# A hybrid decoder layer on one core: start, sample loop and gates reordered, and the last quarter of the second feed-forward product computed in two passes over the tokens

## What is computed

```python
h = rmsnorm(x, norm_mix)
q, k, v, B, C, H, ga, gb = split(h @ w_in)      # 3 x 768, 3 x 512, 2 x 1024 columns
att = dilated_attention(q, k, v, rel_bias)      # 3 groups of 4 heads; samples read caches
b = B * (conv_b + conv3(C * H))
m = sigmoid(ga) * (att @ w_att_out) + sigmoid(gb) * (b @ w_conv_out)
x = x + m @ w_o
x = x + relu(rmsnorm(x, norm_mlp) @ w_ff1) ** 2 @ w_ff2
y = rmsnorm(x, norm_final)
```

## Time and profile before

| | us |
|---|---|
| median of 3 runs | 1695.65 (1692.61 to 1696.15) |
| the profiled execution, its own time | 1697.69 |
| span of the profiled execution | 1695.8 |
| PE busy | 1650.8 (97%) |
| DVE busy | 672.5 (40%) |
| ACT busy | 472.1 (28%) |
| POOL busy | 73.1 (4%) |
| mean granted clock of TensorE | 0.992 of full speed |

### The profile page before, as it was taken

How to read it: one execution, slowest core, us unless ns; L and a number is a source line. 1 busy time by engine, 2 the same in 40 slices (tenths; PEclk the granted TensorE clock), 3 DMA queues, 4 the chain that set the end, 5 groups by cost and what they waited for, 6 DMA issues and landing times.

```text
span 1695.8 us, 28576 instructions
## 1 busy us (share of the span) xinstructions
PE 1650.8 (97%) x10715; PEld 1602.2 (94%) x10715; DVE 672.5 (40%) x1222; ACT 472.1 (28%) x906; POOL 73.1 (4%) x86
## 2 busy tenths in 40 slices
PE   7999999999989999999999999999999999999998
PEld 7999998888978888899999999999999999999998
DVE  6112123344644444323544344333333333333454
ACT  5212123443433443111423331033101321033212
POOL 0430000000000000000122000000000000000011
PEclk9999999999999999999999999999999999999998
DMA  5524554332256765433111111111111111111112
GB/s 174 158 90 129 172 181 123 110 103 85 82 154 171 200 175 147 148 102 108 39 50 37 50 37 50 49 37 49 50 37 49 37 49 40 46 41 46 43 31 106
DMA packets 229017, 152.08 MB, mean 90 GB/s; under 512 B 23870, under 2 KB 219286, under 8 KB 228969
## 3 DMA queue, kind: packets, MB, share of 16 engines
q1 hardware_dynamic: 200412, 120.32, 24.7%
q10 hardware_dynamic: 26268, 28.31, 4.9%
q0 software_dynamic: 2288, 2.80, 0.7%
HBM read 118.32 MB, written 35.43 MB: 91 GB/s over the span
## 4 chain that ended last, share of the span: by engine, by line
PE 86%; issue 3%; DVE 3%; DMA 3%; ACT 2%; SPq 2%; ACTq 1%; DVEq 0%; POOL 0%
PE bank L626 27%; PE bank L627 27%; PE bank L628 27%; ACT wh L1042 1%; PE bank L771 1%; PE bank L740 1%; PE bank L757 1%; PE bank L693 1%; DMA wr<-in_w_conv_out_dram 1%; PE bank L950 1%; DMA xt<-in_x_prompt_dram 1%; DMA xp<-in_x_sample_dram 0%; DMA out_dram<-yt 0%; DMA wr<-in_w_in_dram 0%; SPq L510 0%
## 5 line engine op out<-in xcount | busy, mean ns | idle before, releaser
L626 PE MATMUL bank<-xhi,wh 128*128 128x352 f32 (+1 forms) x1104 | 373.2, 338 | 4.7 <-DVE sga L1811 2.6
L627 PE MATMUL bank<-xlo,wh 128*128 128x352 f32 (+1 forms) x1104 | 362.2, 328 | 0.0
L628 PE MATMUL bank<-xhi,wl 128*128 128x352 f32 (+1 forms) x1104 | 361.8, 328 | 0.0
L1449 DVE TENSOR_TENSOR wl<-wr,wh 128x1024 fp32r<-128x1024 f32 (+1 forms) x134 | 179.7, 1341 | 260.2 <-ACT wh L1042 259.4
L627 PE MATMUL bank<-flo,wh 128*128 128x368 f32 (+1 forms) x768 | 251.7, 328 | 0.0
L627 PE MATMUL bank<-hlo,wh 128*128 128x368 f32 (+1 forms) x768 | 251.4, 327 | 0.0
L626 PE MATMUL bank<-hhi,wh 128*128 128x368 f32 (+1 forms) x768 | 250.6, 326 | 0.3 <-DVE rel L1867 0.3
L626 PE MATMUL bank<-fhi,wh 128*128 128x368 f32 (+1 forms) x768 | 250.5, 326 | 0.0
L628 PE MATMUL bank<-fhi,wl 128*128 128x368 f32 (+1 forms) x768 | 250.1, 326 | 0.0
L628 PE MATMUL bank<-hhi,wl 128*128 128x368 f32 (+1 forms) x768 | 250.1, 326 | 0.0
L1042 ACT ACTIVATE wh<-wr 128x1024 fp32r<-128x1024 f32 (+1 forms) x134 | 136.1, 1015 | 364.8 <-PE bank L628 293.4
(11 more groups left out here) (218 smaller groups left out, 1734.2 us busy)
## 6 DMA issues: line engine op xcount, KB each, us to landing
wr<-in_w_ff_dram SPq DMA_DIRECT2D x64, 512.0 KB, 3.7
wr<-in_w_in_dram SPq DMA_DIRECT2D x46, 512.0 KB, 3.9
d_T<-stg ACTq DMA_DIRECT2D x18, 544.0 KB, 2.8
kvc<-in_cache_kv_g_dram SPq DMA_DIRECT2D x16, 512.0 KB, 5.3
kvc<-in_cache_kv_g_dram SPq DMA_DIRECT2D x32, 256.0 KB, 5.8
d_tm<-tm ACTq DMA_DIRECT2D x12, 512.0 KB, 3.7
d_m<-bb ACTq DMA_DIRECT2D x8, 544.0 KB, 3.0
ml<-d_m SPq DMA_DIRECT2D x8, 544.0 KB, 4.4
```

The costliest lines, as they stand in the source:

```text
L626: pe.matmul(bank[c][:, 0:n], wh[st_.p][:, k, :], a, start=(k == 0), stop=False)
L627: pe.matmul(bank[c][:, 0:n], wh[st_.p][:, k, :], b, start=False, stop=False)
L628: last = pe.matmul(bank[c][:, 0:n], wl[st_.p][:, k, :], a, start=False, stop=(k == nk - 1))
L1449: dve.tensor_tensor(wl[st_.p][:, 0:nk, :], wr[st_.p][:, 0:nk, :], f32(wh[st_.p][:, 0:nk, :]), ALU.subtract).then_inc(w_lo, 1)
```

## The change

Line numbers of the changed kernel are used in the excerpts of its order only; everywhere else a line is one of the kernel before.

**At the start** SP loads the mixing norm's weights as one row of 4 KB. PE spreads it over the partitions by two products of 512 columns with a row of ones that POOL sets (banks 0 and 1), ACT copies one half to `gb` and DVE the other. Three squarings of x move ahead of splits on ACT. The bias tables are multiplied one at a time behind the chunks of step 2, and the constants transposed after chunk 0 of step 3; their copies on ACT and DVE move behind the epilogues of those steps.

```diff
-                sp.dma_start(gb[:], bass.AP(g_mix.tensor, 0, [[0, P], [1, D]])).then_inc(gb_in, 16)
+                sp.dma_start(gb[0:1, :], bass.AP(g_mix.tensor, 0, [[D, 1], [1, D]])).then_inc(gb_in, 16)
...
         keep_warm(WARM[0])
+        pe.wait_ge(gb_in, 16)
+        pe.wait_ge(ones_row, 1)
+        for half in range(2):
+            pe.matmul(bank[half][:], sr[:, 0, :], gb[0:1, 512 * half:512 * half + 512], start=True, stop=True).then_inc(gb_pe, 1)
+        keep_warm(WARM[1])
...
-        tables()
         chunk(Step(1), KD, 2, xhi, xlo)
-        for s in range(2, 6):
+        for c in range(3):
+            chunk(Step(2), KD, c, xhi, xlo)
+            tables(c)
+        chunk(Step(3), KD, 0, xhi, xlo)
+        tables(None)
+        for c in (1, 2):
+            chunk(Step(3), KD, c, xhi, xlo)
...
         square_x(0)
         root_x(0)
+        act.wait_ge(gb_pe, 2)
+        act.activation(gb[:, 0:512], bank[0][:], ACT.Copy).then_inc(gb_c, 1)
         square_x(1)
...
         split_hi(Step(1), KD)
+        square_x(6)
+        square_x(7)
         split_x_hi(3)
-        square_x(6)
+        square_x(8)
         stage_first(0, 0, 1)
         split_x_hi(4)
-        square_x(7)
-        square_x(8)
...
+        dve.wait_ge(gb_pe, 2)
+        dve.tensor_copy(gb[:, 512:D], bank[1][:]).then_inc(gb_c, 1)
+        dve.wait_ge(gb_c, 2)
         scale_x(0)
```

```diff
+                    if g == 2:
+                        pe.wait_ge(cs_ev, 1)
                     pe.wait_ge(pt_d, i * 4 + (8 * g + j))
...
-                pe.wait_ge(s_d, 64)
+                pe.wait_ge(pt_d, 16)
                 for f in range(FC):
-                    last = pe.transpose(bank[3][0:18, f * P:(f + 1) * P], csb[:, f, :], ident[:])
+                    last = pe.transpose(bank[7][0:18, f * P:(f + 1) * P], csb[:, f, :], ident[:])
                 last.then_inc(cs_pe, 1)
-                pe.wait_ge(cs_ev, 1)
...
                     z_terms(f)
+                    bias_scores(g, i, 1)
                 split_lo(st1, KD)
                 prompt_chunk(g, st0, f, 0)
-                bias_scores(g, i, 1)
+                if g < 2:
+                    bias_scores(g, i, 1)
                 prompt_chunk(g, st0, f, 1)
                 bias_scores(g, i, 2)
...
             st0 = Step(S_SAMPLE, (2, b))
+            keys_dve(b, 1)
             split_lo(st0 + 1, KD)
-            keys_dve(b, 1)
...
             query_loads(b)
             gate_b_weights(b)
+            if not last:
+                conv_weights(b + 1)
...
+        def gate(i, p):
+            st_ = Step(S_GATE + 2 * p, (4, i))
+            chunk(st_, KD, 0, xhi, xlo)
+            if isinstance(i, int) and p == 0:
+                turn_sample_out(NB_S - 1)
+            chunk(st_, KD, 1, xhi, xlo)
+            pe.wait_ge(ats_a, 32)
+            pe.wait_ge(res_in[p], i * 32 + 32)
+            pe.wait_ge(res_d, i * 6 + 3 * p)
+            for t in range(TILES):
+                w = rows_of(t)
+                last = pe.transpose(bank[3 + t // 4][:, (t % 4) * P:(t % 4) * P + w], xp[p][0:w, t, :], ident[0:w, 0:w])
+                if t in (3, 7, 8):
+                    last.then_inc(res_pe, 1)
+            chunk(st_, KD, 2, xhi, xlo)
...
             for c, (t0, n) in enumerate(CH):
                 chunk_in(st_, c)
+                if c == 2:
+                    split_hi(st_ + 2, KD)
```

```diff
+        for j in range(KD):
+            weights(W_2[3][:, :, j * P:(j + 1) * P], KD, Step(S_FIRST + j))
+        for j in range(KD):
+            weights(W_2[3][:, :, j * P:(j + 1) * P], KD, Step(S_REST + j))
+            if j >= 5:
+                store(j - 5)
...
+        for j in range(KD):
+            st_ = Step(S_FIRST + j)
+            pe.wait_ge(w_lo, st_.s + 1)
+            for c in range(2):
+                pe.wait_ge(taken[c], st_.s)
+                products(st_, CH_LAST[c], bank[c], (93, 96) if j + c == 0 else None).then_inc(ready, 1 + c)
...
+        pe.wait_ge(taken[1], S_REST)
+        pe.wait_ge(taken[2], S_FIRST)
+        turned = {1: 0, 2: 1, 4: 2, 5: 3, 6: 4, 7: 5}
+        for j in range(KD):
+            st_ = Step(S_REST + j)
+            if j in turned:
+                t = turned[j]
+                pe.wait_ge(yT_d, 2 * KD)
+                if t >= 2:
+                    pe.wait_ge(yt_a, t - 1)
+                    pe.wait_ge(yt_d, t - 1)
+                turn_y(t, range(KD))
+            pe.wait_ge(w_lo, st_.s + 1)
+            if j >= 2:
+                pe.wait_ge(rest_d, j - 1)
+            products(st_, CH_LAST[2], bank[2 - j % 2], None, range(4))
+            if j == KD - 1:
+                pe.wait_ge(ssf_p, 2 * KD - 3)
+                sums(range(FIRST_TILES, TILES), bank[0], ssf, True, False)
+            products(st_, CH_LAST[2], bank[2 - j % 2], None, range(4, KD)).then_inc(ready, 3)
+            if j == 1:
+                pe.wait_ge(ssf_p, KD - 1)
+                pe.wait_ge(taken[0], S_REST)
+                sums(range(FIRST_TILES), bank[6], ssf, True, True).then_inc(yn_pe, 1)
+        pe.wait_ge(yT_d, 3 * KD - 1)
+        pe.wait_ge(rest_d, KD - 1)
+        for t in range(FIRST_TILES, TILES):
+            if t < 8:
+                pe.wait_ge(yt_a, t - 1)
+                pe.wait_ge(yt_d, t - 1)
+            turn_y(t, range(4))
+        pe.wait_ge(sqf_a, 2 * KD)
+        sums(range(FIRST_TILES, TILES), bank[0], sqf[1], False, True).then_inc(yn_pe, 1)
+        pe.wait_ge(rest_d, KD)
+        pe.wait_ge(yT_d, 3 * KD)
+        for t in range(FIRST_TILES, TILES):
+            turn_y(t, range(4, KD))
...
+            dve.tensor_tensor(x, acc[:, 0:n], x, ALU.add).then_inc(y_d, 1)
+            if between:
+                split_lo(between, KD)
+            dve.wait_ge(y_d, e + 1)
+            dve.tensor_scalar(yT[:, j, t0:t0 + n], x, gfc[:, j:j + 1], None, ALU.mult).then_inc(yT_d, 1)
...
+        for j in range(KD):
+            st_ = Step(S_REST + j)
+            t0, n = CH_LAST[2]
+            if j == KD - 1:
+                y_out(5)
+            if j == 2:
+                dve.wait_ge(yn_pe, 1)
+                dve.tensor_scalar(rst[:, 0, 0:FIRST_TILES], bank[6][:, 0:FIRST_TILES], 1.0 / D, EPS, ALU.mult,
+                                  ALU.add).then_inc(yn_d, 1)
+                rstd(yn_d, 1, yr_a, 1, (slice(None), slice(0, FIRST_TILES)))
+            chunk_in(st_, 2)
+            add(j, CH_LAST[2], bank[2 - j % 2], 88 + j).then_inc(rest_d, 1)
+            add_rest(j, t0, n, 88 + j, rest_d, j + 1, st_ + 2 if j + 2 < KD else None)
+            if 2 <= j < KD - 1:
+                y_out(j - 2)
...
+        for j in range(1, KD):
+            pool.wait_ge(sqf_a, j + 1)
+            pool.tensor_tensor(ssf[:, 0:FIRST], sqf[0][:, 0:FIRST] if j == 1 else ssf[:, 0:FIRST], sqf[j % 2][:, 0:FIRST],
+                               ALU.add).then_inc(ssf_p, 1)
...
+            pool.wait_ge(sqf_a, KD + j + 1)
+            pool.tensor_tensor(ssf[:, FIRST:TOK], sqf[0][:, FIRST:TOK] if j == 1 else ssf[:, FIRST:TOK], sqf[j % 2][:, FIRST:TOK],
+                               ALU.add).then_inc(ssf_p, 1)
+            pool.wait_ge(ssf_p, KD - 1 + j)
```

247 lines of the change are left out of this document (132 added, 115 removed).

## The result

| | before | changed |
|---|---|---|
| median, same comparison (us) | 1695.90 (1692.61 to 1697.01, 4 runs) | 1683.04 (1682.76 to 1683.65, 4 runs) |
| ratio | | 0.993 (0.9917 to 0.9944) |
| span of the profiled execution | 1695.8 | 1681.9 |
| PE busy | 1650.8 | 1647.1 |

The change wins 12.9 us at the median and 13.9 in the profiled spans. 1678.9 had been forecast, so 16.8 against 12.9; the time lies inside the range of 1669 to 1688. The page of the changed kernel, part 1, answers to the earlier trace rows: PE's share is 98% now.

What follows compares the result with a forecast made beforehand. It took PE's products as the bound (busy 97% of the span). Its terms, 2.4 - 2.8 - 7.0 - 7.1 - 2.6 + 0.3, made -16.8 us: 1680.9 in the profiled execution's terms, 1678.9 at the median; range 1669 to 1688.

Steps and rivals of the forecast that it cites:

- Third attention group: Third attention group: PE's waits for `cst` and the second score bias go, some given back at the third biases; -2.8 us.
- The entry to the gates: Before the gates: moved chunk covers the late residual, so waits and the low clock behind them go; -7.1 us.
- Gate steps: Gate steps: ScalarE's split of the next gate's weights goes ahead of the third sigmoid, removing most `sga` waits; -2.6 us.
- The last quarter: Last quarter in two passes: shorter tail against added turns, a stand and low clock; 50.8 us against 50.5, +0.3.
- the start: Start: spread behind the warm-up makes squaring 5.2 us late; 1.0 returns from squarings, 1.8 from the tables' clock; +2.4.
- the samples: Sample loop: key copies ahead of splits -4.7, convolution weights a sample ahead -2.2, other terms nearly cancelling; -7.0 us.
- The term of 0.94 us per beat: Sample loop: PE's next transposes, held by splits ahead of the key copy, come 0.94 us earlier per body; five bodies, -4.7.
- The sample loop: Rival: loads or ScalarE's exponents set the loop's beat, so only sample 1's 2.2 us is won; 1683.6 us, chance 0.13.
- one engine later: Rival: the change does little, as waits reappear where VectorE's copies stand behind other splits; 1694 us, chance 0.03.
- More is won: Rival: PE does not stand in step 2, its clock holds, the start loses nothing; 1672 us, chance 0.17.
- The slower rival: Last quarter's second pass falls to half clock and stays there, taking 33 us more; 1711.9 us, chance 0.04.
- The weights: Rival: the last quarter's second pass hangs on weight loads of 7.3 us, 1.4 more per step; 1690 us, chance 0.08.

Runs made afterwards that it cites:

- e6: The changed kernel with the bias tables and constants in one piece again, their copies back ahead of step 2; 1681.14 us.
- e7: The changed kernel with the spread of the mixing norm's weights ahead of the warm-up, and 6 warm-up products instead of 28; 1673.26 us.
- e12: The changed kernel with the old broadcast of the mixing norm's weights and 6 warm-up products; 1674.56 us.
- e4: The changed kernel with each sequence's convolution weights loaded at its own head again; 1690.78 us.
- e3: The changed kernel with the split of the gate weights ahead of the key copies again, on ScalarE and VectorE; 1689.73 us.
- e9: The changed kernel with ScalarE's root for token tiles 0 to 5 ahead of its weight split for step 4 of the second pass; 1679.25 us.
- e10: The changed kernel with spread ahead of 6 warm-up products, ScalarE's root ahead of its split, first two tables each ahead of the chunk that waited; 1670.01 us.
- e1: The changed kernel with the mixing norm's weights loaded by the old broadcast DMA, without spread and copies; 1673.85 us.

## Why the prediction was right and wrong

**What held.** The bound, the sign and the mechanisms of five terms. Third attention group: -2.4 for -2.8. The entry to the gates: -7.4 for -7.1; the chunk that was moved ahead covers the residual, and the low clock behind the stand went with it. Gate steps: -2.1 for -2.6. The last quarter: the stand ahead of tile 2's turn was put at 2.8 and is 2.5 in the list of waits (the chain was put at 6.4 us after step 2's end, though the pieces with a price make 5.6 and the root has none, and less the 3.5 that step 3 covers it is 2.9; by the trace the chain is 5.9, from 1645.60 to 1651.48); the low clock behind it was put at 1.7 us lost, and 8 us at 0.79 are 1.7. That the clock fell there at all is chance: in e6, e7 and e12 it did not behind the same stand. The second pass with its turns and sums takes 40.1 us (1631.52 to 1671.67), where the terms gave 40.5. The new width costs nothing, as was chosen: 64 products of each kind at 0.147 apart, although a weight load takes 0.19. Only the tail was short: 10.2 us instead of 9.5.

**What failed: the start.** "5.2 us late", "of that, 1.0 comes back" and 1.8 at the tables gave +2.4; it is +6.5. Three parts of it were off:
- The spread ended at 15.60 and not at 14.4. The two products took 1.98 us, close to the 1.8 chosen; it was the warm-up that ran longer, 9.24 instead of the 8.17 of the earlier trace rows. The second squaring began 6.25 late and the first product 6.23 late. The length of the warm-up is chance from execution to execution: in the seven other traces with this start the first product comes at 25.9 to 27.1, 5.1 to 6.3 late.
- "1.0 comes back" did not. PE's longest wait for scaled x rose from 1.0 to 1.5. In the kernel before, a stretch at low clock (21.5 to 25) had lain over the same chain of ACT and DVE and hidden it; a faster PE only waits for it. In e7, at clock 1.00 there, PE waits 0.96 us for x tile 3, and the tile's transposes begin 3.15 us after the first product, as in the kernel before, where PE did not wait for it.
- "After them the clock was 0.84, 1.8 us of work lost; with products around each table I expect that back" was true of the clock and false of the time. The clock is 1.00 there, but PE now waits 0.6 for ACT's emptying of bank 2 and 0.8 for the weights of step 2, which the tables had covered; in e6, with them back, the stretch takes 1.2 us less, low clock included. The price of the removed cover was missing from the sum, and so was the long issue that comes with the spread and makes the second of these waits.

**What was undersized: the samples**, -9.2 for -7.0. The term of 0.94 us per beat measured 1.16, which is half of the miss. The other half lies before the third sample's scores, where the sum has no clock term: the kernel before ran at 0.60 in 502 to 506, behind waits for `kTs` of 1.1 and 1.7 us, and the changed kernel at 1.00. Of the variants e4 alone has low clock there. And the split of the term was wrong. It gave 4.7 to the order of copies and splits and 2.2 to the convolution weights, "in the second sample". By e3 and e4 each half alone leaves the loop at nearly its old beat: the waits stand in two engines' lists, and whichever is left sets the time.

**The total.** In the traces the sum missed by 2.9 us: 4.1 at the start, 2.2 the other way in the samples, and 1.0 in the four others together. That the time came as near as it did is in part luck, since two errors cancel. The other 1.0 of the miss at the median (3.9) is that the gain was read from one trace of the kernel before and taken off the median.

**The rivals.** The sample loop did not keep its beat (23.82 us for 24.98), and the waits did not come back one engine later to the extent of 1694. "More is won" was wrong for the changed kernel: PE did stand in step 2. e9 and e10 show what it would have taken. The slower rival, a second pass at the low clock, fell: the granted clock is 1.00 from 1630 to 1648, with transposes and sums among the products and low only behind the stand. The rule named there (the Trainium skill, TensorE: Matmul & The Clock Gate, Part 4: PE-mode transpose), that transposes do not count as busy work in the same way, is not borne out by this trace either, at this share of transposes; what transposes without products among them would do, it does not show. The weights did not hold up the second pass: the list of waits shows none there.

## What to carry to other kernels

Before an operation is moved, ask what stands under it: work of another engine that it covers becomes a wait when it goes, even if the operation itself costs the same elsewhere. An operation put behind a fixed warm-up is as late as that warm-up, whatever it costs; the question is what could run first. Where two engines' lists each hold a late step for the same consumer, undo them one at a time in an experiment: neither half is worth its share alone. And where a stand is followed by the low clock in one trace, look at other traces with the same stand before that clock is put into a sum or credited to an edit.

## What the runs showed of the hardware that was not expected

The warm-up ran at two speeds in windows whose granted clock reads 1.00. Kernel before and changed kernel, windows of the same stretch (counts behind PE are records begun):

```profile
4.40:8.00 3.60, 3.60 (x17) 3.60 (x18) 0.80 (x5) 1.16 (x3) 0.00 (x0) 1.00 0.91 281
8.00:12.00 4.00, 4.00 (x38) 4.00 (x38) 1.29 (x1) 2.01 (x3) 0.00 (x0) 1.00 1.07 390
```

```profile
4.40:8.00 3.60, 3.54 (x16) 3.54 (x17) 0.80 (x5) 1.18 (x3) 0.00 (x0) 1.00 0.98 335
8.00:12.00 4.00, 4.00 (x29) 4.00 (x28) 0.00 (x0) 0.00 (x0) 0.00 (x0) 1.00 1.06 409
```

Records begin 0.213 us apart at first and 0.112 later; the first pace held for 15 records before and for 26 in the changed kernel, which is the whole 1.07 us by which its warm-up was longer. The 1.00 is no reading at first: the clock entries of the two traces begin at 7.90 and 10.19 us, just where the pace doubles, and time without an entry counts as full clock. In the changed kernel four such records take 1.06 us at a granted clock of 0.50 (from 19.54) and 0.61 at 1.00 (from 24.67), so the first pace is that of the lower level, and where the rise falls differs between executions: 8.0 to 10.5 in the seven other traces with the changed kernel's start.

A stand of the same length did not always cost the clock. In both traces of the changed kernel and in e1 to e4 a stretch at 0.50 followed the 2.5 us ahead of tile 2's turn; in e6, e7 and e12, with the same stand, none did (e7, the stretch from 3.5 us ahead of the turn on):

```profile
1639.00:1647.00 8.00, 5.54 (x41) 5.30 (x40) 6.96 (x10) 3.04 (x5) 2.38 (x2) 1.00 0.44 135
```

A DMA issue on ACT's queue takes 0.39 us at the median of the 93 in a run, and about ten take 0.8 to 1.1, but one to three in a run took 1.25 to 2.9. The two longest of the changed kernel fell on the same instructions in both of its profiled executions. The first of them is the 64th recorded instruction of ACT's list in all eleven traces with the spread, and long in all of them; with the broadcast the same issue is the 63rd, and short in all three. The stretch around it (53 to 59, changed kernel) holds one packet of a queue of the kind "instruction" (DMA view), but the like stretch of e1 (46 to 52) holds one too and has no long issue, so that packet alone does not explain it. What does was not tried.

```profile
q14 instruction: 1, 0.01, 0.5%
```
